# Two units side by side at the start of a two-layer decoder trunk, with half-slot loads

## The reference

```python
h = rms_norm(x, attn_norm_w[i])
proj = h @ w_in[i]
dq, dk, dv, cq, ckv, krope, xq, gates = split(proj)
# A: differential attention, 8 heads, rope on dq and dk
# B: latent attention, 8 heads: rms_norm(cq) @ mla_w_uq, rms_norm(ckv) @ mla_w_ukv, rope
mh = rms_norm(mem, mem_norm_w[i])
mk, mv = split(mh @ w_mem_kv[i])          # C: cross attention into memory, 4 heads of 128
g_a, g_b, g_c = split(sigmoid(gates))
x = x + (g_a * y_a + g_b * y_b + g_c * y_c) @ w_out[i]
x = x + (silu(f_gate) * f_up) @ w_down[i]  # on rms_norm(x, ffn_norm_w[i])
```

## Time and profile before

| | |
|---|---|
| median of three runs | 1941.99 us |
| the profiled execution | 1942.73 us |
| its span (first to last instruction) | 1940.9 us |
| TensorE matmuls | 1931.2 us (100%) |
| TensorE weight loads | 1627.2 us (84%) |
| VectorE / ScalarE / GpSimd | 1066.6 (55%) / 933.8 (48%) / 1077.9 (56%) |
| moved by the DMA engines | 242.80 MB, mean 125 GB/s |

### The profile page before, as it was taken

How to read it: one execution, slowest core, us unless ns; L and a number is a source line. 1 busy time by engine, 2 the same in 40 slices (tenths; PEclk the granted TensorE clock), 3 DMA queues, 4 the chain that set the end, 5 groups by cost and what they waited for, 6 DMA issues and landing times.

```text
span 1940.9 us, 28787 instructions
## 1 busy us (share of the span) xinstructions
PE 1931.2 (100%) x9298; PEld 1627.2 (84%) x9298; DVE 1066.6 (55%) x1904; ACT 933.8 (48%) x1661; POOL 1077.9 (56%) x1439
## 2 busy tenths in 40 slices
PE   9999999999999999999999999999999999999998
PEld 8888888888888888888888888888888888888887
DVE  5767888887555333321155778888875543333111
ACT  6454766667444322233344456676673442222332
POOL 5764454454655555567755645445446555555674
PEclk9999999999999999999999999999999999999999
DMA  6446433334532322233344463343354322222232
GB/s 240 120 127 237 119 117 115 118 115 137 203 133 87 108 96 90 98 109 100 103 142 139 139 214 121 110 121 118 107 190 162 121 98 97 97 97 92 82 91 94
DMA packets 167349, 242.80 MB, mean 125 GB/s; under 512 B 55890, under 2 KB 74066, under 8 KB 166740
## 3 DMA queue, kind: packets, MB, share of 16 engines
q1 hardware_dynamic: 142960, 204.79, 32.9%
q10 hardware_dynamic: 24292, 36.75, 5.6%
HBM read 208.71 MB, written 32.77 MB: 124 GB/s over the span
## 4 chain that ended last, share of the span: by engine, by line
PE 93%; POOL 3%; issue 2%; DMA 1%; ACT 1%; DVE 1%; SPq 0%; ACTq 0%; POOLq 0%; DVEq 0%
PE proj L684 23%; PE proj L686 23%; PE proj L685 23%; POOL w_lo L641 3%; PE score L684 2%; PE score L686 2%; PE score L685 2%; PE flip L753 2%; PE score L910 1%; PE score L908 1%; PE score L739 1%; PE score L738 1%; PE score L912 1%; PE score L911 1%; PE score L733 1%
## 5 line engine op out<-in xcount | busy, mean ns | idle before, releaser
L641 POOL TENSOR_TENSOR w_lo<-raw,w_hi 128x256 fp32r<-128x256 f32 x1372 | 1073.9, 815 | 842.6 <-ACT w_hi L1233 842.4
L684 PE MATMUL proj<-h_hi,w_hi 128*128 128x512 f32 x1552 | 611.9, 394 | 0.2 <-POOL w_lo L641 0.2
L686 PE MATMUL proj<-h_hi,w_lo 128*128 128x512 f32 x1552 | 605.3, 390 | 0.0
L685 PE MATMUL proj<-h_lo,w_hi 128*128 128x512 f32 x1552 | 604.2, 389 | 0.0
L1233 ACT ACTIVATE w_hi<-raw 128x1024 fp32r<-128x1024 f32 x344 | 363.2, 1057 | 193.9 <-DMA raw<-in_w_down 53.2
L686 PEld LDWEIGHTS proj<-h_hi,w_lo 128*128 128x128 f32 x1552 | 291.3, 188 | 62.5
L685 PEld LDWEIGHTS proj<-h_lo,w_hi 128*128 128x128 f32 x1552 | 291.7, 188 | 57.5
L684 PEld LDWEIGHTS proj<-h_hi,w_hi 128*128 128x128 f32 x1552 | 291.5, 188 | 57.8 <-issue 0.6
L684 PE MATMUL proj<-hid_hi,w_hi 128*128 128x512 f32 x330 | 129.0, 391 | 0.0
L686 PE MATMUL proj<-hid_hi,w_lo 128*128 128x512 f32 x330 | 128.5, 389 | 0.0
L685 PE MATMUL proj<-hid_lo,w_hi 128*128 128x512 f32 x330 | 128.4, 389 | 0.0
(11 more groups left out here) (459 smaller groups left out, 3228.0 us busy)
## 6 DMA issues: line engine op xcount, KB each, us to landing
raw<-in_w_in SPq DMA_DIRECT2D x224, 256.0 KB, 2.9
raw<-in_w_gate_up SPq DMA_DIRECT2D x176, 256.0 KB, 2.8
raw<-in_w_down SPq DMA_DIRECT2D x96, 192.0 KB, 2.4
gate_in<-gate_scratch ACTq DMA_DIRECT2D x48, 256.0 KB, 4.0
gate_scratch<-gate_out ACTq DMA_DIRECT2D x44, 256.0 KB, 2.5
raw<-in_w_mem_kv SPq DMA_DIRECT2D x32, 256.0 KB, 2.9
raw<-in_w_o_diff SPq DMA_DIRECT2D x32, 256.0 KB, 2.8
raw<-in_w_out SPq DMA_DIRECT2D x32, 256.0 KB, 2.8
```

Of the source, the lines that this page charges most:

```text
L641: ins = g.tensor_tensor(w_lo[s][:, cols], raw[s % 2][:, cols], w_hi[s][:, cols].bitcast(F32), ALU.subtract)
L684: mm(o, hi[:, c:c + width], rh, start=start and k == 0, stop=False)
L685: mm(o, hi[:, c:c + width], rl, start=False, stop=False)
L686: ins = mm(o, lo[:, c:c + width], rh, start=False, stop=stop and k == n - 1)
```

## The change

WARM goes from 13 to 9. Units 0 and 1 of layer 0 run side by side: each tile of x goes through both, with the first halves of both slots for tiles 0 to 3 and the second halves for 4 to 7. The low weights of unit 1 come last, together. x is loaded in eight tiles, the first on ScalarE's queue with the first half of slot 1; memory is queued ahead of slot 2, the row tiles of x later. VectorE writes memory's high parts in layer 0. ScalarE takes the squares of memory around slot 2. The rope cosines move behind the low parts of the last cross head, and the store of the tables behind two slot copies. The core of the diff:

```diff
-WARM = 13
+WARM = 9
@@ sync
-                slot(l, "N", 0, 0, *whole(w_in, l, T_XQ))
-                    for quarter in range(1, 4):
-                        load_x(quarter)
-                slot(l, "N", 0, 1, *gate(l, GATES_N))
+                    sp.dma_start(raw[0][:, 0:4 * P], tiles(w_in, l, 0, 4, T_XQ)).then_inc(in_first[0], 16)
+                    for k in range(1, 4):
+                        load_x(k)
+                    for half, tile in enumerate((T_XQ, T_GATE + GATES_N)):
+                        sp.sem_inc(raw_full[half], 16)
+                        sp.dma_start(raw[half][:, 4 * P:], tiles(w_in, l, 4, 8, tile)).then_inc(raw_full[half], 16)
+                    for k in range(4, KD):
+                        load_x(k)
+                    sp.dma_start(memT[:, :, :], mem[:, :, :]).then_inc(in_mem, 16)
                 slot(l, "N", 0, 2, *whole(w_in, l, T_CQ))
-                    sp.dma_start(memT[:, :, :], mem[:, :, :]).then_inc(in_mem, 16)
-                    load_x_row(0)
-                    load_x_row(1)
                 slot(l, "N", 0, 3, *gate(l, GATES_N + 1))
-                    load_x_row(2)
-                    load_x_row(3)
+                    for t in range(3):
+                        load_x_row(t)
                 slot(l, "N", 0, 4, *whole(w_mem_kv, l, 0))
+                    load_x_row(3)
@@ gpsimd
+            pool.wait_ge(first_high, 2)
+            (two pieces of w_lo[1], columns 0:4 * P)
+            pool.wait_ge(slot_hi.sem, slot_hi.before + 2)
+            pool.wait_ge(slot_lo.sem, slot_lo.at(0, "N", 0, 1))
+            low(1, 4 * P)
@@ tensor, first_layer
+                units = ((0, proj[0][:, :]), (1, score[1][:, :]))
+                for k in range(4):
+                    high(k)                  # a matmul of each unit; k == 0 waits for first_high 1, then 2
+                    if k:
+                        low_rows(k - 1)      # a matmul of each unit
+                pe.wait_ge(first_low, 1)
+                low_weights(0, 0, 4)
+                for k in range(4, KD):
+                    high(k)
+                    low_rows(k - 1)
+                low_rows(KD - 1)
+                pe.wait_ge(slot_lo.sem, slot_lo.at(l, "N", 0, 1))
+                low_weights(0, 4, KD).then_inc(slot_done.sem, 1)
+                pe.wait_ge(slot_lo.sem, slot_lo.at(l, "N", 0, 2))
+                low_weights(1, 0, KD).then_inc(slot_done.sem, 1)
@@ scalar
+            act.dma_start(xT[:, 0, :], x[:, 0, :]).then_inc(in_x[0], 16)
             act.dma_start(gains[:, 0:GAIN_COLS], gain_cols[:, :]).then_inc(in_gain, 16)
+            act.dma_start(raw[1][:, 0:4 * P], (gate tile, rows 0 to 3)).then_inc(in_first[1], 16)
+            first_half(0)
             act.wait_ge(in_gain, 16)
             first_tile(0)
-            first_tile(1)
-            first_slot(0)
-            for k in range(2, KD):
+            first_half(1)
+            for k in range(1, 4):
                 first_tile(k)
-            first_slot(1)
+            for s in range(2):
+                second_half(s)
+            for k in range(4, KD):
+                first_tile(k)
@@ scalar, new_layer, l == 0
+                    act.wait_ge(in_mem, 16)
+                    memory_squares(0, 4)
                     first_slot(2)
-                    memory_tiles(l)
-                    row_squares(x_row, in_x_row, x_ss, x_squared, 0, 2)
+                    memory_squares(4, KD)
                     first_slot(3)
                     (store of the first gate, loads of lambda and positions)
-                    memory_squares(0, 4)
-                    row_squares(x_row, in_x_row, x_ss, x_squared, 2, NT)
+                    row_squares(x_row, in_x_row, x_ss, x_squared, 0, 3)
+                    split_ahead(l, "N", 0, 1)
+                    row_squares(x_row, in_x_row, x_ss, x_squared, 3, NT)
                     root(x_ss, x_root, x_squared, NT, x_rooted)
-                    split_ahead(l, "N", 0, 1)
-                    memory_squares(4, KD)
                     split_ahead(l, "N", 0, 2)
@@ scalar, stage A
-                    (wait for rope_ready, store of the tables)
                 rms(l, "A", 0, 0)
                 (four high parts of the latent queries)
                 split_ahead(l, "A", 0, 3)
                 split_ahead(l, "A", 0, 4)
+                    (wait for rope_ready, store of the tables)
@@ vector
-                if k == 1:
-                    (w_lo[0] of the whole slot 0)
+                if k == 0:
+                    (wait for first_high 1, w_lo[0] of columns 0:4 * P, raises first_low)
+                if k == 3:
+                    (wait for slot 0's high part, w_lo[0] of columns 4 * P on)
@@ vector, new_layer, l == 0
+                    ve.wait_ge(in_mem, 16)
+                    memory_tile(0)
                 for k in range(KD):
+                    if l == 0 and k < KD - 1:
+                        memory_tile(k + 1)   # tensor_scalar: mem_hi[k + 1] = memT[k + 1] * gain
+                    if l == 0 and k == 6:
+                        (wait for unit 1, copy of the first gate)
                     (mem_lo[k])
@@ vector, stage A
+                memory_low(l, i)
+                cross_low(l, i)
                 if l == 0:
                     rope_cosines()
-                memory_low(l, i)
-                cross_low(l, i)
```

More of the change, by code:

```diff
@@ L376, in build_trunk @@
         in_x_row = [sem(f"in_x_row{t}") for t in range(NT)]
-        in_x = [sem(f"in_x{quarter}") for quarter in range(4)]
+        in_x = [sem(f"in_x{k}") for k in range(KD)]
+        in_first = [sem(f"in_first{s}") for s in range(2)]
+        first_high, first_low = sem("first_high"), sem("first_low")
         pre_act = sem("pre_act")
@@ L635, in _, with low @@
             total = slot_lo.total * DEPTH
-            def low(s):
-                for c in range(0, KD * P, 2 * P):
+            def low(s, first=0):
+                for c in range(first, KD * P, 2 * P):
                     cols = slice(c, c + 2 * P)
@@ L642, in low @@
                 ins.then_inc(slot_lo.sem, 1)
[L644 removed]
+            pool.wait_ge(first_high, 2)
+            for c in range(0, 4 * P, 2 * P):
+                cols = slice(c, c + 2 * P)
+                g.tensor_tensor(w_lo[1][:, cols], raw[1][:, cols], w_hi[1][:, cols].bitcast(F32), ALU.subtract)
+            pool.wait_ge(slot_hi.sem, slot_hi.before + 2)
+            pool.wait_ge(slot_lo.sem, slot_lo.at(0, "N", 0, 1))
+            low(1, 4 * P)
+            for s in range(2, 4):
                 pool.wait_ge(slot_hi.sem, slot_hi.before + s + 1)
[L646 to L647 removed]
                 low(s)
@@ L999, in first_layer @@
                 l = 0
-                w, o = ring("N", 0), proj[0][:, :]
-                pe.wait_ge(slot_hi.sem, slot_hi.at(l, "N", 0, 1))
+                units = ((0, proj[0][:, :]), (1, score[1][:, :]))
+                pe.wait_ge(first_high, 1)
                 pe.wait_ge(kv_copied.sem, kv_copied.at(l, "C"))
+                pe.wait_ge(oc_used.sem, oc_used.at(l, "E"))
                 def high(k):
                     pe.wait_ge(pair_hi.sem, pair_hi.at(l, "A", 0, k + 1 - KD))
-                    mm(o, w_hi[w][:, k * P:(k + 1) * P], h_hi[:, k, :], start=k == 0, stop=False)
+                    for u, o in units:
+                        if k == 0 and u:
+                            pe.wait_ge(first_high, 2)
+                        if k == 4:
+                            pe.wait_ge(slot_hi.sem, slot_hi.at(l, "N", 0, u + 1))
+                        mm(o, w_hi[u][:, k * P:(k + 1) * P], h_hi[:, k, :], start=k == 0, stop=False)
@@ L1021, in first_layer, with low_weights @@
[L1021 to L1025, removed]
+                    for u, o in units:
+                        mm(o, w_hi[u][:, k * P:(k + 1) * P], h_lo[:, k, :], start=False, stop=False)
+                def low_weights(u, first, last):
+                    o = units[u][1]
+                    for k in range(first, last):
+                        ins = mm(o, w_lo[u][:, k * P:(k + 1) * P], h_hi[:, k, :], start=False, stop=k == KD - 1)
+                    return ins
```

54 lines of the change are left out of this document (28 added, 26 removed).

## The result

The changed kernel took 1945.96 us (median of 17 runs, 1944.69 to 1947.84), the kernel before 1942.11 beside it (17 runs, 1941.66 to 1944.21): ratio 1.0019, interval 1.0013 to 1.0026. That is a slowdown, though within the 0.2% that the prediction called no change. The profiled execution took 1945.41 with a span of 1943.6, 2.7 more than the 1940.9 of before. So the trace holds 2.7 of the 3.9 us: the profiled execution of after is the third fastest of its 17, and that of before (1942.73) lies above its median.

What follows compares the result with a forecast made beforehand. TensorE was taken as busy throughout, so only an earlier start or removed stalls could pay. Terms 0.86 + 0.3 + 0.2 + 0.8 = 2.16, rounded to 2.2, from the 1941.99 median gave 1939.8 us, range 1938.7 to 1942.4.

Steps and rivals of the forecast that it cites:

- Start, -0.86: First two units: first real matmul at 6.3, dense from 7.8, both units ending at 18.25 against 19.11: -0.86 us.
- the start does not move: Rival at the start: queues share the transfer rate, gate's half lands at 7.5, only 1.3 us goes: 1940.7; chance 0.07.
- Clock, the rival with 0.20: Rival at the start: TensorE's clock rises late after a thin stretch, 2.75 us of work lost: 1942.5; chance 0.20.
- Warm-up costs nothing by itself: Before the first real matmul: cutting 13 warm-ups to 9 costs no time itself and permits the early start.
- Memory and slot 2 cost nothing: Before the third unit: memory lands at 14.3, slot 2 is ready at 17.85, wanted at 18.25: no cost.
- Behind it, -0.3 and -0.2: After the start: earlier slot 4 copy brings forward the low part awaited at 40.42, -0.3; memory's squares summed sooner, -0.2.
- Rope cosines, -0.8: Last cross head's attend matmuls: with the cosines behind the low parts, the stall before 114.51 goes: -0.8 us.
- Late store of the tables at 0: Table store moved to near 126.4: VectorE's overwriting begins 1.2 us later with 1.7 to spare, cost nothing (bounds 0 and 1.2).

Runs made afterwards that it cites:

- reordered start: After with memory as before, SyncE issuing the gate's half, 11 warm-ups, two query-unit x tiles first, ScalarE's tile 1 before the gate's half: +1.06 us over before (1.0006).
- memory part alone: Kernel before with only memory's load ahead of slot 2, VectorE scaling it, its squares around slot 2, later row tiles and row root: +2.59 us (1.0016).

## Why the prediction was wrong, step by step

- *Start, -0.86: wrong, +2.29 at the third unit and 2.65 in the time alone.* The gate's half was to land at 6.5 and landed at 7.9. The forecast charged it for the bytes ahead of it at the rate of a full stream; the third transfer on a queue of its own, with SyncE's loads beside it, took 6.2 us. Dense matmuls began at 9.25 instead of 7.8: +1.45. The rival "the start does not move" had the cause and too small a price (7.5, and no gain lost elsewhere). x tiles every 0.64 us do not hold either: VectorE's low part of a tile took 1.22 us beside a split of GpSimd (reordered start) where the shortest there took 0.74.
- *Clock, the rival with 0.20: it came, by another path.* It was to rise late; it rose, fell after the hole, and 3.4 us at half rate cost 8 matmuls x 0.20 = 1.6 us. 18.25 + 1.45 + 1.6 = 21.3, measured 21.40.
- *Warm-up costs nothing by itself: right* (-0.46 in the kernel before).
- *Memory and slot 2 cost nothing: right where it looked, wrong where it did not.* Slot 2 was split by 18.1 and no matmul waited for it. But the forecast never followed SyncE's queue behind slot 2. The row tiles moved behind slot 3, the fourth behind slot 4, and neither the gap in the transfers nor the row root was priced. Alone this step cost 2.6 us, as much as the start. The memory itself came as forecast (issued at 6.28, landed 8.4 us later, at 14.7; forecast 14.3).
- *Behind it, -0.3 and -0.2: wrong sign.* ScalarE was to copy slot 4 at about 24.4 and copied it at 28.99, since its load was issued 3.1 us later than before and landed just then; the forecast looked at ScalarE's order alone. The wait at 40.42 did go, since TensorE was later than the split. The sum of memory's squares was to be 0.2 us earlier and is waited for 1.36. The forecast read "with the squares done by 19 they start at 28", and overlooked that these additions stand on VectorE behind the row root, which moved from 28.3 to 32.6.
- *Rope cosines, -0.8: the mechanism right, the size 0.62 alone.* In after only 0.2 arrives (43.54 - 40.42 = 3.12, then 117.43 - 114.51 = 2.92). Part of it goes into the new wait of 0.23 on the low part of the query's sum at 113.24; why ScalarE's square for it comes 0.7 us later than the shift was not followed.
- *Late store of the tables at 0: right.* It was issued at 128.55, and no wait of TensorE follows.

The sum of the working was -2.2; the span says +2.7 and the medians +3.9. The clock's fall is in 13 of 17 runs, so that rival was no rare accident; but the runs of after without it average 1945.6, so it is the smaller part of the loss.

## What to carry to other kernels

When loads are reordered, write down for each queue what each later load now stands behind, and for each engine what each later instruction stands behind, down to the first matmul that needs them; here the losses of the memory part were two places behind the instruction that was looked at. When a cure moves the matmul it was meant for and not the end, look for a second chain that ends at the same place, and cure both in one kernel before judging either. And undo the parts one by one: two of three parts were losses here, and one of these, repaired, most likely a gain. A single trace can show the rarer course of a kernel; the mean clock of every run tells which course the others took.

## Of the hardware, not expected

- The clock's rise at the start differs from execution to execution and is no fixed count of warm-ups: it was at 5.0 us in one profile (13 warm-ups in after) and as late as 14.5 in another (after with the additions moved), with the same instructions on TensorE as in after, where it was 6.8. The fall at 10.2 to 10.5 came in the four profiled executions that had 9 warm-ups, a hole of 1.5 to 1.95 us, and a rise at 6.8 to 7.1. It did not come in the profile with 13 warm-ups, a hole of 2.07 and the rise at 5.0, though 7 of 11 runs of that kernel have the mean clock of a fall. So what a hole costs depends on the execution as well. Of such holes the Trainium skill says, page "TensorE: Matmul & The Clock Gate", section "HAM oscillation — how this bites in real kernels", that a wait for a transfer between bursts can bring the low clock back. The waits of its example are about 3 to 5 us; here 1.5 to 1.95 did it, and 2.07 once did not.
- VectorE and GpSimd block each other. An operation on 128x4 elements took 0.17 us in the kernel before and 0.67 while GpSimd split (memory part alone), and one split of 0.73 took up to 2.9 us in after. The Trainium skill, page "SBUF — State Buffer", section "SBUF: two separate sides", calls the pair of ports that they share "an exclusive lock", held for a whole instruction; these durations agree. Keeping them apart at slot 2's split gained nothing. On the row root it mattered: ScalarE's root was ready at 32.5 both in after and in the run with row tiles 0 and 1 ahead, but there the four steps took 2.68 us in place of 0.99, and C0 came 0.79 later.
- The time to landing does not follow the bytes: ScalarE's three transfers of after (x tile 0, the gains, the gate's half), issued at about 0.75, 1.2 and 1.7, landed after 4.0, 4.4 and 6.2 us, and the one with 36 KB (the gains) was no faster than the x tile with 256.
